# An expert mixture's weight streaming: the two blocks that take the place of x are loaded inside the branch, after two gathers, and no longer in front of it

## What is computed

```python
scores = jax.nn.sigmoid(h.astype(F32) @ w_router.astype(F32))
...                                   # best group of 4, then the top 2 experts inside it, gates
for e in range(N_EXPERTS):
    he = jax.nn.silu(h @ w_gate[e]) * (h @ w_up[e])
    y = y + gates[:, e:e + 1] * (he @ w_down[e])
```

## Time and profile before

| what | value |
|---|---|
| median of 3 runs | 1136.79 us |
| span of the profiled execution | 1133.3 us |
| TensorE matmuls busy | 1026.4 us, 91% |
| VectorE busy | 498.7 us, 44% |
| ScalarE busy | 330.5 us, 29% |
| GpSimd busy | 108.2 us, 10% |
| moved by DMA | 225.34 MB, mean 199 GB/s |
| of it on SP's queue (q1) | 153.29 MB |
| blocks loaded into x in the whole kernel | 12 of 1024 KB, median 19.1 us from issue to landing |

### The profile page before, as it was taken

One profiled execution on the slowest core, in us unless ns is written; L12 is line 12 of the kernel. 1 busy time (PEld: TensorE's weight loads), 2 busy tenths in 40 slices (PEclk: granted clock), 3 DMA queues, 4 the chain that ended last, 5 costly groups with the idle time before them and its releaser, 6 DMA issues.

```text
span 1133.3 us, 25508 instructions
## 1 busy us (share of the span) xinstructions
PE 1026.4 (91%) x10346; PEld 678.7 (60%) x10346; DVE 498.7 (44%) x1261; ACT 330.5 (29%) x875; POOL 108.2 (10%) x136
## 2 busy tenths in 40 slices
PE   7999997699998499999899999989999958999975
PEld 3687454566664367777788887456555535666632
DVE  1581134322222636497536663666623352222227
ACT  0102114133333323223334332155421132333320
POOL 0010000210000300000211111301000002100021
PEclk9999998699999699999999998899999968999997
DMA  9653205999996632122322242575353089999944
GB/s 348 260 85 60 114 38 199 320 356 369 370 410 238 204 149 75 38 90 74 91 69 74 72 139 72 190 287 202 126 219 149 19 326 291 370 375 374 397 134 182
DMA packets 79982, 225.34 MB, mean 199 GB/s; under 512 B 9312, under 2 KB 50320, under 8 KB 61296
## 3 DMA queue, kind: packets, MB, share of 16 engines
q1 hardware_dynamic: 64304, 153.29, 37.3%
q0 software_dynamic: 11968, 57.71, 15.5%
q10 hardware_dynamic: 3584, 12.58, 2.9%
HBM read 201.57 MB, written 40.86 MB: 214 GB/s over the span
## 4 chain that ended last, share of the span: by engine, by line
PE 85%; DMA 4%; issue 4%; DVE 4%; ACT 1%; POOL 0%; DVEq 0%; POOLq 0%; SPq 0%; ACTq 0%
PE bank L1290 16%; PE bank L1194 10%; PE bank L1466 9%; PE bank L1314 8%; PE bank L1382 6%; PE bank L1563 4%; PE bank L1401 3%; PE bank L1272 2%; PE bank L1438 2%; DMA xkept<-x 1%; PE bank L1816 1%; PE bank L1841 1%; PE bank L1205 1%; PE bank L1543 1%; DMA work<-yrows,rowi 1%
## 5 line engine op out<-in xcount | busy, mean ns | idle before, releaser
L1194 PE MATMUL bank<-ring,cat 128*128 128x512 f32 x256 | 112.6, 594 | 1.3 <-ACT cat L2002 1.3
L1466 PE MATMUL bank<-xT,ring 128*128 128x288 f32 x448 | 110.9, 407 | 0.0
L1466 PEld LDWEIGHTS bank<-xT,ring 128*128 128x128 f32 x448 | 84.6, 190 | 23.8 <-issue 1.1
L1290 PE MATMUL bank<-ring,work 128*32 128x128 f32 (+1 forms) x1344 | 81.5, 315 | 1.7 <-DVE work L2441 1.7
L1194 PEld LDWEIGHTS bank<-ring,cat 128*128 128x128 f32 x256 | 47.5, 190 | 57.2 <-issue 57.2
L2451 DVE TENSOR_TENSOR work<-work,bank 128x192 f32<-128x192 f32 x32 | 11.3, 354 | 155.4 <-ACT work L1968 155.4
L2460 DVE COPY work<-bank 64x512 f32<-64x512 f32 x64 | 44.0, 688 | 67.2 <-PE bank L1314 66.7
L1290 PEld LDWEIGHTS bank<-ring,work 128*32 128x32 f32 (+1 forms) x1344 | 57.4, 121 | 24.3 <-issue 12.0
L1382 PE MATMUL bank<-xT,ring 128*128 128x288 f32 x256 | 63.1, 407 | 0.0
L1968 ACT ACTIVATE work<-bank 128x192 f32<-128x192 f32 x32 | 10.6, 332 | 161.4 <-PE bank L1290 161.4
L1382 PEld LDWEIGHTS bank<-xT,ring 128*128 128x128 f32 x256 | 48.3, 190 | 13.5 <-issue 0.4
(11 more groups left out here) (451 smaller groups left out, 1890.8 us busy)
## 6 DMA issues: line engine op xcount, KB each, us to landing
ring<-in_stream_dram SPq DMA_DIRECT2D x63, 1024.0 KB, 8.6
work<-in_stream_dram SPq DMA_DIRECT2D x16, 1024.0 KB, 18.8
cat<-in_stream_dram SPq DMA_DIRECT2D x16, 1024.0 KB, 21.1
by_batch<-in_pages_dram SPq DMA_DIRECT2D x128, 128.0 KB, 2.4
x<-in_stream_dram SPq DMA_DIRECT2D x12, 1024.0 KB, 19.1
xT<-in_stream_dram SPq DMA_DIRECT2D x12, 1024.0 KB, 16.3
yrows<-work ACTq DMA_DIRECT2D x32, 384.0 KB, 7.6
lnp<-in_ln_dram POOLq DMA_DIRECT2D x4, 1024.0 KB, 15.5
```

The costliest lines, as they stand in the source:

```text
L1194: i = pe.matmul(bank(n)[0:ROWS[tile], :], cat[:, k, tok(tile)], slot(w[k // 4], 4, 512)[:, k % 4, :], start=(k == 0), stop=(k == KC - 1))
L1290: i = pe.matmul(by_half[rows * q:rows * q + rows, :, to:to + width], xgT[:, e % 2, k, at:at + rows], w[:, :, width * q:width * q + width], ...
L1466: i = pe.matmul(bank(n + s)[:, 0:nn], slot(w, KC, 256)[:, k, P * (m % 2):P * (m % 2) + P], xT[:, k, a:a + nn], start=(k == 0), stop=(k == ...
```

## The change

`AHEAD` also leaves out the two places in x, so it is the list of blocks 5 to 8, and the two lines that loaded blocks 9 and 10 in front of the branch are gone. The loop of the sparse way begins at `AHEAD[-1] + 1`, which is now 9 and not 11: blocks 9 and 10 are loaded there, behind the wait for the first two gathers and in front of blocks 11 and 12. The waits on `x_kept` and `acc_and_gates` stay where they are. In the crowded way the x blocks are neither loaded nor waited for.

```diff
 SPARE = [("work", 0), ("work", 1), ("cat", 0), ("cat", 1), ("x", 0), ("x", 1), ("xT", 0), ("xT", 1)]
 NSPARSE = NSLOT + len(SPARE)
-AHEAD = [NSLOT + i for i, (home, _) in enumerate(SPARE) if home != "xT"]
+AHEAD = [NSLOT + i for i, (home, _) in enumerate(SPARE) if home not in ("x", "xT")]
@@
                     take(sp, job(f"{layer}.mT{LAST}", 1))
                     sp.wait_ge(x_kept, 16 * NT * (layer + 1))
                     sp.wait_ge(acc_and_gates, NT * (layer + 1))
-                    for j in AHEAD[4:6]:
-                        load_spare(layer, j)
                     flag = is_crowded(sp, layer)
```

## The result

The changed kernel takes 1139.79 us, the median of 12 runs (1137.49 to 1146.78), against 1135.36 us for the kernel before in 12 runs. The ratio is 1.0037, with a 95% interval of 1.0023 to 1.0050: some 4.2 us slower, between 2.6 and 5.7. The forecast was +4.3 us, 1141.1 us, on the base of 1136.79. The profiled execution of the changed kernel is the slowest of the twelve, which has to be kept in mind when its span is read.

A forecast was written before the change was run, and what follows sets the result against it. TensorE was taken to bound the expert stages, with DMA engines nearly as full. Late weights of 2.8 + 1.5 us, with 0 for gathers, SP and moved uses, gave +4.3 us: 1141.1 us, range 1135.2 to 1145.5.

The forecast's parts named there:

- step 5: Experts 11 and 12: 2.10 MB moved into the full stretch make weights late, 2.8 us in layer 1, 1.5 in layer 0.
- Every block from 11 on 3 to 5 us later: Sign the forecast is right: in the expert stages, every block from 11 on lands 3 to 5 us later.
- Step 4: Stage entry: first gather lands no sooner, taken as 0, with bounds of 0 and 1.0 to 1.15 us a layer.
- a first gather under 4.5 us: Sign at the stage entry: if the first gather lands in under 4.5 us, the claim of 0 gain is wrong.
- step 2: In the branch: x issues precede xT's, 0.80 us of SP, nobody waits; drained x blocks are claimed one part earlier.
- Steps 1 to 3: Stage entry to expert 3: x issues move into the branch, 0.80 us of SP; blocks some 15 us early; cost 0.
- B: Rival, expert stages: late weights plus TensorE's lower clock after the wait, 3.1 us more in both layers, 1144.2 us; chance 0.15.
- C: Rival, experts 11 and 12: gaps absorb 1.5 of the 2.10 MB, no expert waits, 1136.8 us; chance 0.17.
- D: Rival, stage entries: nothing waits and first gathers land 1.15 + 1.0 us sooner, 1134.6 us; chance 0.10, stronger form 0.03.

## Why the prediction was right

**The mechanism (step 5) held.** The empty stretch before the gathers, the later landings, and TensorE's waits at experts 10 and 11 are in the profile of the changed kernel, in every repetition, and in that layer alone which is changed. They go away when 2.10 MB are taken out later, or when only one block is moved.

**Its size held in part by luck.** The waits came to 4.4 to 4.5 us in the two profiles of the changed kernel; predicted were 2.8 + 1.5 = 4.3. But layer 1 was put at 2.8 and gave 2.0 and 2.4, and layer 0 at 1.5 and gave 2.5 and 2.0. The forecast took the delay at one block in each layer, the one that was least ahead of its use. The delay is not one number. Line L936 again, block 31 of layer 1, the kernel before first, the changed kernel second:

```profile
L936 SPq DMA_DIRECT2D work<-in_stream_dram x1: 467/467/467, 1004.8 to 1004.8; - x1
DMA to landing us min/median/max: 23.3/23.3/23.3
...
L936 SPq DMA_DIRECT2D work<-in_stream_dram x1: 440/440/440, 1015.3 to 1015.3; - x1
DMA to landing us min/median/max: 28.9/28.9/28.9
```

It landed at 1028.1, 5.0 us ahead of expert 10's group at 1033.12, and at 1044.2 in the changed kernel, where the first gather is issued 11.1 us later: 5.0 us of delay, and nothing left of the lead. Block 34, where the forecast had 5.0 us, landed 3.5 us later (1054.8 - 11.1 = 1043.7, against 1040.2), and block 37 2.3. So layer 1 came out below its 2.8 us, and TensorE's wait began at expert 10 already. In layer 0 block 37 landed 3.7 us later, as forecast. But blocks 31 and 34 landed 6.6 and 6.0 us later than in the second profile of the kernel before, which had them 5.0 and 3.3 us ahead, so TensorE waited at experts 10 and 11, where the forecast had not looked, and block 37 was then in time. "Every block from 11 on 3 to 5 us later" was too narrow: blocks 14 to 37 of layer 1 landed 2.3 to 7.6 us later.

The price of a byte was about right for the early part of the stage and too high at the end, as four blocks moved showed: 0.26 to 0.30 MB/us at blocks 21 to 25, near 0.4 from block 34 on. At 0.39 the 3.5 us of block 34 are 1.4 MB (an estimate), so gaps took up some 0.7 of the 2.10 MB; the forecast had 0.56. That layer 0 would come out cheaper, as its gaps are larger, did not hold: the waits are alike.

**Step 4, the first gather,** was taken at 0, with 1.0 to 1.15 us as the other end. It is near 0 to 0.6 in layer 0 and 1.0 in layer 1 (4.1 to 4.2 us in the changed kernel against 5.2 to 5.6), so by the prediction's own sign, a first gather under 4.5 us, the step failed in layer 1. Part of the gain is spent at once where the entry of before was a quick one: TensorE's first group of layer 1 took 7.35 to 7.6 us with the change and 6.89 in the first profile of before, but 8.4 to 8.5 in two others. What is left of it is taken up by the waits: expert 11's group of layer 1 began 1.4 us later than before, counted from the first gather's issue, though the waits there sum to 2.0. The reason given for 0, that the x blocks had drained (step 2), was not quite true. Block 10 of layer 1 in the kernel before:

```profile
L936 SPq DMA_DIRECT2D x<-in_stream_dram x1: 435/435/435, 924.9 to 924.9; - x1
DMA to landing us min/median/max: 12.8/12.8/12.8
```

It landed at 937.7, some 4 us after the first gather was issued (933.64). The Trainium skill's fit (DMA: Bandwidth & Descriptors, "Anatomy of one DMA") gives an estimate of 2.9 us for these rows. No run reached it: the quickest first gather without x blocks took 4.09 us.

**Steps 1 to 3** held otherwise: SP's issues moved to 214.43, no engine waited for SP, and experts 3 and 4 waited for nothing.

**The rivals.** B, the clock after a wait: not in the changed kernel, whose waits came in pieces of 0.6 to 1.6 us, but seen with four blocks moved, where the group after waits of 1.9 and 2.8 us took 1.7 us more. C and D, absorbed or faster, are out for two blocks in both layers; for one block C is what happens, and with layer 1 alone changed the time does not tell the kernel from the one before, though the waits are there. What no rival named is that the entries vary from one execution to the next by more than the gather's gain.

## What to carry to other kernels

Before a transfer is moved off a quiet stretch, find the points later on where the data is little ahead of its use, and compare lead and delay at each of them, not only at the least lead; if the DMA engines are full until then, the moved bytes arrive there as a wait, less the lead. Their price changes along the way (here 0.3 MB/us while gathers pass, 0.4 at the end). It is a threshold: 1 MB moved cost nothing, 2 MB 2.7 to 4.2 us, 4 MB 12 us. And a transfer that has all but drained when the urgent one starts does it little harm, here up to 1 us a layer: putting it off to protect the urgent one wins little and can lose more.

## What the runs showed of the hardware

Gathers of 4 KB rows and block loads side by side moved 292 GB/s, with every engine counted as busy, where block loads alone moved 424. So overlapping the two won nothing here (the block issued 2.6 us sooner landed 1.2 us later), and a busy share near 1 does not say how much is carried. A gather that starts beside 2.10 MB of loads took 8.8 and 9.7 us from issue to landing, beside no loads 4.1 to 5.3. And the granted clock at the entry of a stage rose at a point that moved between executions of the same program. Windows of layer 1 in the two profiles of the kernel before, whose first gathers were issued at 933.64 and 932.93:

```profile
944.00:949.00 5.00, 5.00 (x97) 3.93 (x94) 0.96 (x5) 0.67 (x2) 0.00 (x0) 1.00 1.02 328
```

```profile
944.00:949.00 5.00, 5.00 (x82) 3.49 (x78) 0.04 (x1) 0.00 (x0) 0.00 (x0) 0.74 1.04 305
```

The same 96 matmuls took 6.89 us in the first and 8.52 in the second.
